# Moving a ring of six weight tiles 64 bytes lower in SBUF, in a one-core hybrid diffusion layer

## The reference, cut to what matters

```python
h = rmsnorm(x, norm1_g) * (1 + sc1) + sh1
z = h @ w_in                                   # r k v, codes, q k v of attention, two gates
mixed = sigmoid(ga) * (y_a @ w_out_a) + sigmoid(gb) * (y_b @ w_out_b)
x = x + g1 * (mixed @ w_out)
h2 = rmsnorm(x, norm2_g) * (1 + sc2) + sh2
u, gte = split(h2 @ w_ffn_up, 2)
x = x + g2 * ((gelu(dwconv3(u, conv_ffn)) * gte) @ w_ffn_down)
```

## The kernel before, in words

| tensor | first word | bytes mod 128 | bytes mod 256 |
|---|---|---|---|
| `hH`, `mixH`, `h2H` | 2720 | 0 | 128 |
| `hL` | 33440 | 0 | 128 |
| `h2L` | 12960 | 0 | 128 |
| `factH` / `factL` | 23200 / 27040 | 0 | 128 |
| `qkv_hi` / `qkv_lo` | 45728 / 26784 | 0 | 128 |
| ring, before | 47056 | 64 | 64 |
| ring, after | 47040 | 0 | 0 |

## Time and profile before

### The profile page before, as it was taken

One profiled execution on the slowest core, in us unless ns is written; L12 is line 12 of the kernel. 1 busy time (PEld: TensorE's weight loads), 2 busy tenths in 40 slices (PEclk: granted clock), 3 DMA queues, 4 the chain that ended last, 5 costly groups with the idle time before them and its releaser, 6 DMA issues.

```text
span 2509.1 us, 50765 instructions
## 1 busy us (share of the span) xinstructions
PE 2382.1 (95%) x21658; PEld 1964.0 (78%) x21658; DVE 1296.3 (52%) x2077; ACT 725.6 (29%) x1189; POOL 657.8 (26%) x283
## 2 busy tenths in 40 slices
PE   5899999999999998889999998999999999999997
PEld 4777878788888887888745687888888888888886
DVE  4575657527568667895543323634333433443344
ACT  5273644634455553333300001201100110011002
POOL 2022020111211111222000244434344444444341
PEclk9999999999999999999989998999999999999999
DMA  6313111022266786676423310111111111111112
GB/s 281 109 35 106 55 60 62 28 95 76 93 193 193 202 230 191 196 204 183 154 75 115 119 35 26 34 34 43 35 42 34 43 34 43 34 42 37 40 34 93
DMA packets 224561, 234.53 MB, mean 93 GB/s; under 512 B 143922, under 2 KB 178866, under 8 KB 222898
## 3 DMA queue, kind: packets, MB, share of 16 engines
q1 hardware_dynamic: 199090, 229.55, 28.4%
q10 hardware_dynamic: 25344, 3.15, 0.8%
HBM read 173.80 MB, written 57.02 MB: 92 GB/s over the span
## 4 chain that ended last, share of the span: by engine, by line
PE 81%; DVE 8%; issue 3%; ACT 2%; DMA 2%; SPq 1%; ACTq 1%; POOL 1%; DVEq 0%; POOLq 0%
PE PS L878 20%; PE PS L879 20%; PE PS L880 20%; PE PS L1354 6%; PE PS L1022 3%; PE PS L994 2%; DVE buffer L2081 2%; PE PS L1008 1%; DVE buffer L2080 1%; PE PS L996 1%; DMA buffer<-in_w_ada_first 1%; ACTq L1729 1%; PE PS L1074 1%; PE PS L1164 1%; PE PS L1326 1%
## 5 line engine op out<-in xcount | busy, mean ns | idle before, releaser
L878 PE MATMUL PS<-buffer,buffer 128*128 128x512 f32 (+1 forms) x2784 | 997.5, 358 | 10.2 <-DVE buffer L1976 3.4
L879 PE MATMUL PS<-buffer,buffer 128*128 128x512 f32 (+1 forms) x2784 | 987.8, 355 | 1.7 <-issue 1.7
L880 PE MATMUL PS<-buffer,buffer 128*128 128x512 f32 (+1 forms) x2784 | 987.8, 355 | 0.0
L878 PEld LDWEIGHTS PS<-buffer,buffer 128*128 128x128 f32 x2784 | 525.6, 189 | 97.3 <-issue 17.0
L880 PEld LDWEIGHTS PS<-buffer,buffer 128*128 128x128 f32 x2784 | 525.6, 189 | 78.8 <-issue 2.1
L879 PEld LDWEIGHTS PS<-buffer,buffer 128*128 128x128 f32 x2784 | 525.9, 189 | 75.2 <-issue 1.0
L2366 POOL TENSOR_TENSOR buffer<-buffer,buffer 128x1024 fp32r<-128x1024 f32 x76 | 184.0, 2421 | 816.8 <-PE PS L880 510.4
L2309 DVE SCALAR_TENSOR_TENSOR buffer<-PS,buffer,buffer 128x512 f32<-128x512 f32 (+1 forms) x264 | 158.5, 655 | 151.4 <-PE PS L880 151.4
L2367 POOL TENSOR_TENSOR buffer<-buffer,buffer 128x1024 fp32r<-128x1024 f32 x76 | 194.1, 2554 | 6.0
L2285 DVE TENSOR_SCALAR buffer<-buffer,buffer 128x1281 f32<-128x1281 f32 x22 | 34.8, 1582 | 286.6 <-ACT buffer L1810 286.6
L1810 ACT ACTIVATE buffer<-PS 128x512 f32<-128x512 f32 (+1 forms) x66 | 30.0, 529 | 504.3 <-PE PS L880 504.3
(11 more groups left out here) (228 smaller groups left out, 2796.9 us busy)
## 6 DMA issues: line engine op xcount, KB each, us to landing
buffer<-in_w_up SPq DMA_DIRECT2D x44, 512.0 KB, 3.3
buffer<-in_w_in SPq DMA_DIRECT2D x42, 512.0 KB, 5.2
ops_kept<-buffer SPq DMA_DIRECT2D x40, 512.0 KB, 4.6
buffer<-ops_kept SPq DMA_DIRECT2D x80, 256.0 KB, 3.4
buffer<-in_w_ada SPq DMA_DIRECT2D x32, 512.0 KB, 6.3
buffer<-rkv_kept SPq DMA_DIRECT2D x120, 128.0 KB, 3.3
buffer<-in_w_down SPq DMA_DIRECT2D x22, 512.0 KB, 3.3
buffer<-in_x SPq DMA_DIRECT2D x20, 512.0 KB, 7.6
```

The source lines that it names most:

```text
L878: mm(out, w_hi, x_hi, start=start, stop=False)
L879: mm(out, w_hi, x_lo, start=False, stop=False)
L880: return mm(out, w_lo, x_hi, start=False, stop=stop)
```

## The change

The first word of the ring is rounded down to a multiple of 32 words. All six tiles, `SI`, `S0` and the two matrices placed from `RING` move 16 words (64 bytes) down. Tensors placed from `WORDS` (`ada_ring`, `silu`, `gate_w`, `sd_tok`) stay. No instruction, size, wait or order changes.

```diff
-        RING = WORDS - 6 * KB * P
+        RING = (WORDS - 6 * KB * P) // 32 * 32
         ring = Space(RING)
         raw = [ring(KB, P) for _ in range(2)]
         hi, lo = [None, None], [None, None]
```

## The result

The changed kernel takes 2533.03 us (median of 4 executions, 2531.36 to 2534.76) against 2513.86 us before: 1.0076 times as long, 95% interval 1.006 to 1.0092, so 19.2 us slower. The forecast was 2515, range 2498 to 2526, and "no difference" the likeliest. The slower rival of the prediction is what happened, in its kind and in most of its size.

A forecast was written before the change was run, and what follows sets the result against it. TensorE's matmuls, busy 2382.1 of 2509.1 us, were taken as the bound: count times pace. Tile terms of -2.4, +1.8 and +1.6 made +1.0 us; carried to the median 2514.5 this gave 2515.5, stated as 2515, range 2498 to 2526.

The forecast's parts named there:

- no difference: Whole kernel: time within about 0.3%, 7.5 us, of the kernel before, too close to tell apart; chance 0.55.
- slower rival: Ring's split matmuls: a third pace at the new place, 233 ns at 512 columns; +27 us, 2542; chance 0.16.
- small terms: Work beside the ring's split matmuls: float32 stage, GpSimd rounding, loads, solve; about nothing expected, bounds 3 us each way.
- plain float32: `mix_block` reading `raw`: 592 ns for 512 columns at either place of the weights, so 0 change.
- 0.1 us sooner: GpSimd's rounding into the ring, 2403 ns against 2362 at attention's place: each split tile ready 0.1 us earlier, hidden.
- the moved solve: VectorE solve that moves with `RING`, 26.3 us of work: no change expected, bound a tenth either way, 2.6 us.
- the sum, if the moved ring goes at attention's pace: Ring's split matmuls: straight tile 13.78 us, against 13.82 or 13.71 in its two patterns; together +1.0 us; chance 0.42.
- Faster: Ring's split matmuls: gain at 512 columns without the loss at 256; -10 us, 2505, or 2496 at most; chance 0.30.
- Nothing moves: Ring's split matmuls: paces belong to the stage, not the place, and both patterns come back; 2514.5; chance 0.12.

## Why the prediction was wrong

**The bound and the place of the effect were right.** Time in these stages is the count of matmuls times their pace, and the change acts on the pace alone. The small terms came as said: plain float32 at 429 ns from start to start, as before, the rounding at 2397 for 2403, hidden (the prediction's "0.1 us sooner" for each tile is 0.04 by its own row, and did not come), and in the changed kernel the moved solve, between 940 and 1006 us:

```profile
L2081 DVE TENSOR_TENSOR buffer<-buffer,buffer 128x31 f32<-128x31 f32 (+15 forms) x31 | 13.7, 442 | 1.1
L2080 DVE TENSOR_TENSOR buffer<-buffer,buffer 128x31 f32<-128x31 f32 (+15 forms) x31 | 11.6, 375 | 1.0
```

25.3 us here for 26.3 in the earlier trace rows, with one instruction fewer in the window; its bound of 2.6 us was not used.

**The step that failed** is "the sum, if the moved ring goes at attention's pace". It took attention's projections for the model of the moved ring because both are at a multiple of 128 bytes. But the table of places has attention's weights at the inputs' own remainder modulo 256 (128), and the moved ring at 0: the distance to the inputs is 0 for the one and 128 for the other, and it is this distance that decides. In place of 13.78 us a tile took 14.00 to 14.04, and all starts of the feed-forward block together went from 229.1 to 232.9 ns at 512 columns, where 226.7 was forecast for the settled pace. The run with the ring at attention's distance gave 13.78 us a tile and 1.0003, where the prediction had worked out 13.78 and +1 us: the working was sound and its premise was not met by the change. When it says that the pace "differs with nothing but the weights' place that I can name", its own table of places had the distance to the inputs to name. The text names the risk in the slower rival, "if the remainder modulo 256, or the distance to the inputs, is what counts", and gave it 0.16. The range ended at 2526, below the case.

**The slower rival's size.** It priced the whole ring at 233 ns (21 us), with 119.6 at 256 columns (6 us): +27. By stages 19.5 us were measured. Both of its terms were somewhat too large. Averaged over all starts of the feed-forward block without a longer gap, in the two traces, 512 columns went up by 3.8 ns (229.1 to 232.9) where it took 4.2, and 256 columns by 1.9 (116.2 to 118.1) where its 6 us mean 2.4. In that block this makes 15.0 us, and 12.2 were measured: the longer gaps between its matmuls add up to 2.8 us less than before. The pace alone is thus worth some 22 us in the whole ring, and no sum had in it that the gaps give back some of it, as they do in this pair of traces.

**The other rivals.** Faster (226.7 at 512 columns and the old pace at 256): no multiple of 64 bytes gave that pair. Distances 0 and 64 have the best pace for one size and the worst, or all but the worst, for the other; only distance 240 comes near it (226.7 or 228.3 ns in turn, and 117.3), and its time is not measurably shorter. *Nothing moves*, which went by the SBUF page of the Trainium skill ("SBUF: two separate sides": TensorE's port waits for no other): the port of TensorE may wait for no other engine, and still its two kinds of reads, weights and inputs, have a pace that hangs on where they lie against each other; the measurement decides. That page's 16 byte line (Specifications) does not tell the places apart either: every place tried here is a multiple of 16 bytes, and distances 16 bytes apart (224 and 240) have 233.3 and some 227 to 228 ns.

**What is shown and what is open.** Shown: the pace goes with the distance between split weights and inputs and not with the remainder of either, the same for three ways to reach distance 0 and two each to reach 64 and 128. That only the remainder of the distance counts is shown in part. The three ways to distance 0 have the ring the same 177152 bytes above `hH`; but attention has its pace with weights at 172032 and 96256 bytes from `hH`, and the eight blocks of a tile, whose distance changes by 4608 bytes from one to the next, all go at 680 ns for three. All these differ by multiples of 512 bytes, and all distances tried lie between 0 and 240 of one stretch of 256. So the pace may repeat every 256 bytes, as this text counts, or every 512; that 240 is nearly as good as 0 speaks for 256, but no run decides it. Not settled either: why. The run with `hi` at 0 and `lo` at 192 rules out that each gap depends only on the pair being loaded and read. Open too is why there is more than one pattern at one distance (192, 128, 240) and what makes a kernel pass from one to the other.

## What to carry to other kernels

A comparison inside a trace is worth what its two sides have in common: write down every remainder and distance in which the new place differs from the one that stands for it, not only the one that the change is named after. In a stretch where TensorE is at 100% with weights and inputs both read from SBUF in fp32r, the relative start of the two modulo 256 bytes was worth 0.6 to 0.9% of this kernel between the good distances (0, 192, 240) and the bad (32, 64, 128, 224), with no wait, count or clock to show it; look at start to start times in the timeline, and over several tiles, since one tile may not be typical. Keep weights and inputs at equal remainders, or at a distance that was measured, and expect a change to any tensor placed below to move it.

## What the runs showed of the hardware that was not expected

The pace of fp32r matmuls with a weight load each repeats to a nanosecond: three of 512 columns take 680 ns at distance 0, 687 in the kernel before and 697 to 700 at 32, 64, 128 and 224, three of 256 between 340 and 360, at a granted clock of 1.00. The best paces at 256 columns (113.3 and 113.8 ns) come with 229 and 233 at 512, and the best at 512 (226.7) comes with the worst at 256 (119.6) at distance 0. Plain float32 matmuls with weights from the same ring (line 1354, 512 columns) start 429 ns apart in the kernel before and in the changed one. And with weights and inputs at distance 0, it made no difference whether both were at a multiple of 128 bytes or 64 bytes past it, as the table of places counts (13.78 us a tile both ways): an aligned start had no worth of its own here.
